# State-space loop of a hybrid decoder: TensorE adds the real part of the turned products, the fraction stays at the head of a tile, sample products come last

## The reference

```python
bu_re = einsum("btgc,gpc->btgp", u, bb_re)        # inputs to states
bu_im = einsum("btgc,gpc->btgp", u, bb_im)
s_t   = a * s_(t-1) + bu_t                        # complex, a = mag * exp(i * phi), by associative_scan
y     = einsum(s_re, c_re) - einsum(s_im, c_im) + d_skip * u
out   = gelu(y) * sigmoid(gelu(y) @ w_glu + b_glu)
```

## Time and profile before

| | |
|---|---|
| median of the runs | 3801.35 us (3799.45 to 3801.61) |
| the profiled execution | 3798.16 us, its span 3796.3 us |
| PE busy | 2867.0 us (76% of the span), 10568 instructions |
| DVE busy | 2406.9 us (63%), 3337 instructions |
| POOL busy | 1986.9 us (52%) |
| ACT busy | 656.7 us (17%) |
| the state-space loop | first fraction in the loop's form at 43.05 us, last y started at 355.92 us |
| VectorE's eight scans a tile (L1367), 128 in all | 88.8 us, 762 ns each |

### The profile page before, as it was taken

How to read it: one execution, slowest core, us unless ns; L and a number is a source line. 1 busy time by engine, 2 the same in 40 slices (tenths; PEclk the granted TensorE clock), 3 DMA queues, 4 the chain that set the end, 5 groups by cost and what they waited for, 6 DMA issues and landing times.

```text
span 3796.3 us, 30116 instructions
## 1 busy us (share of the span) xinstructions
PE 2867.0 (76%) x10568; PEld 1645.9 (43%) x10568; DVE 2406.9 (63%) x3337; ACT 656.7 (17%) x1576; POOL 1986.9 (52%) x1620
## 2 busy tenths in 40 slices
PE   4555996777666778898986788888877687666667
PEld 2223773333222326665753456665644342222222
DVE  7997077767775555666466675665456765555563
ACT  6664021101010111221011112221010111000000
POOL 5886025566656554344465453344355556555652
PEclk8777998998888999999998889998988899888888
DMA  2001459999999999999999999999999999999997
GB/s 98 14 12 70 138 241 410 425 422 423 426 419 422 427 427 427 420 411 417 426 427 422 427 421 420 408 420 421 426 427 422 418 411 427 427 427 427 427 427 316
DMA packets 197787, 1407.03 MB, mean 371 GB/s; under 512 B 21984, under 2 KB 26336, under 8 KB 26864
## 3 DMA queue, kind: packets, MB, share of 16 engines
q0 software_dynamic: 166064, 1208.62, 76.2%
q1 hardware_dynamic: 31296, 196.39, 12.6%
q10 hardware_dynamic: 288, 0.18, 0.0%
HBM read 1401.86 MB, written 3.24 MB: 370 GB/s over the span
## 4 chain that ended last, share of the span: by engine, by line
DMA 41%; PE 25%; POOL 15%; DVE 11%; issue 6%; ACT 2%; POOLq 0%; ACTq 0%; DVEq 0%
DMA arena<-in_v_dram,arena 25%; PE ps L704 16%; DMA arena<-in_u_dram,arena 11%; PE ps L626 7%; POOL arena L567 5%; DMA W<-in_slabs_dram 5%; POOL arena L556 4%; DVE arena L1532 3%; POOL arena L494 1%; POOL arena L496 1%; DVE X L1564 1%; POOL arena L472 1%; POOL arena L500 1%; PE ps L716 1%; DVE arena L1443 1%
## 5 line engine op out<-in xcount | busy, mean ns | idle before, releaser
L704 PE MATMUL ps<-arena 128*128 128x512 f32 x3584 | 1805.1, 661 | 650.8 <-DMA arena<-in_v_dram,arena 490.3
L1532 DVE CUSTOM_DVE_ANT_0 arena<-arena,HN 128x2048 f32<-128x2048 f32 x576 | 1311.1, 2291 | 1082.5 <-DMA arena<-in_u_dram,arena 1082.3
L567 POOL DMA_INDIRECT arena<-in_v_dram,arena x576 | 870.2, 1511 | 1202.4 <-PE ps L704 861.1
L704 PEld LDWEIGHTS ps<-arena 128*128 128x128 f32 x3584 | 736.3, 212 | 1686.6 <-issue 939.1
L556 POOL DMA_INDIRECT arena<-in_u_dram,arena x576 | 838.4, 1456 | 505.6 <-DVE arena L1532 192.6
L626 PE MATMUL ps<-HT,W 128*128 128x160 f32 (+2 forms) x3520 | 515.1, 309 | 42.6 <-DMA W<-in_slabs_dram 42.2
L626 PEld LDWEIGHTS ps<-HT,W 128*128 128x128 f32 x3520 | 483.0, 196 | 83.3 <-DMA W<-in_slabs_dram 47.7
L1095 ACT ACTIVATE arena<-arena 128x4 f32<-128x4 f32 x144 | 29.6, 205 | 2026.8 <-DVE arena L1532 2026.7
L1564 DVE SCALAR_TENSOR_TENSOR X<-arena,X 128x2048 f32<-128x2048 f32 x128 | 300.9, 2351 | 69.7 <-DMA arena<-in_v_dram,arena 39.3
L626 PE MATMUL ps<-arena,W 128*128 128x160 f32 (+2 forms) x1440 | 238.8, 329 | 18.0 <-DMA W<-in_slabs_dram 18.0
L626 PEld LDWEIGHTS ps<-arena,W 128*128 128x128 f32 x1440 | 213.7, 197 | 46.4 <-DMA W<-in_slabs_dram 19.9
(11 more groups left out here) (230 smaller groups left out, 1937.2 us busy)
## 6 DMA issues: line engine op xcount, KB each, us to landing
W<-in_slabs_dram SPq DMA_DIRECT2D x168, 1024.0 KB, 10.1
arena<-in_u_dram,arena POOLq DMA_INDIRECT x576, 15.0
arena<-in_v_dram,arena POOLq DMA_INDIRECT x576, 14.0
GB<-in_norms_dram SPq DMA_DIRECT2D x7, 1024.0 KB, 14.6
arena<-in_s_bc_dram SPq DMA_DIRECT2D x32, 128.0 KB, 2.1
X<-in_x_dram SPq DMA_DIRECT2D x3, 1024.0 KB, 7.2
GB<-in_keys_dram SPq DMA_DIRECT2D x2, 1024.0 KB, 10.5
out_y_dram<-HN SPq DMA_DIRECT2D x2, 1024.0 KB, 10.1
```

Source lines behind the costliest of these rows:

```text
L567: pool.indirect_dma_start(ring[:, HALF + r, :], None, experts_v[n // LAYER_ROUNDS], bass.IndirectOffsetOnAxis(ap=GI[:, at:at + 1], axis=0) ...
L704: mm = nc.tensor.matmul(ps[:, ACC_BANK + c, :], diag[:, slot, :], ring[:, HALF + r, BANK * c:BANK * (c + 1)], start=first and r == 0, stop ...
L1532: V.tensor_tensor_reduce(ring[:, r, :], ring[:, r, :], HN[:, tile_of(n), :], 1.0, 0.0, ALU.mult, ALU.add, A8[:, n % TURN, r:r + 1]).then_i ...
```

## The change

In the recurrence's input the real part was the sum of two products, added by VectorE. Now VectorE only makes the two products (M[0], M[1]) and TensorE adds them by two products with the identity into the PSUM banks where re stood; VectorE scans the real part from PSUM. The imaginary part is subtracted and scanned first, in SBUF. The order of the four turned products changes accordingly. `s5_bur` is now raised behind the scans from PSUM and not behind the four products. TensorE's `s5_out_part` is split: token products first, without the wait for the sample states, then the new sums of the next tile, then the gate sums, and the sample products last, behind the wait for `s5_bsd`. The fraction keeps its place at the head of the tile. The two scan results move from M[1] and M[3] to M[0] and M[3].

```diff
@@ TensorE
-            def s5_out_part(k, h):
+            def s5_sums(k):
+                pe.wait_ge(s5_turned, k + 1)
+                for e in range(2):
+                    nc.tensor.matmul(ps[:, e, :], ident[:], M[0][:, 2 * e:2 * e + 2, :], start=True, stop=False)
+                    mm = nc.tensor.matmul(ps[:, e, :], ident[:], M[1][:, 2 * e:2 * e + 2, :], start=False, stop=True)
+                mm.then_inc(s5_sum, 1)
+
+            def s5_out_tokens(k, h):
                 pe.wait_ge(s5_dd, k + 1)
                 pe.wait_ge(s5_cn, k + 1)
                 pe.wait_ge(s5_p, k + 1)
-                pe.wait_ge(s5_bsd, k + 1)
                 pe.wait_ge(s5_yg, k)
...
+            def s5_out_samples(k, h):
+                pe.wait_ge(s5_bsd, k + 1)
                 for n in range(2):
...
             s5_in_part(0, 0)
+            s5_sums(0)
             s5_in_part(0, 1)
-            s5_out_part(0, 0)
+            s5_out_tokens(0, 0)
+            s5_sums(1)
+            s5_out_samples(0, 0)
             for i in range(1, KT // 2):
                 for h in range(2):
                     s5_in_part(i, h)
-                    s5_out_part(2 * i + (h - 1), 1 - h)
+                    s5_out_tokens(2 * i + (h - 1), 1 - h)
+                    s5_sums(2 * i + h)
                     gate_sums(2 * i + (h - 2))
-            s5_out_part(KT - 1, 1)
+                    s5_out_samples(2 * i + (h - 1), 1 - h)
+            s5_out_tokens(KT - 1, 1)
+            s5_out_samples(KT - 1, 1)
             gate_sums(KT - 2)
@@ VectorE, s5_tile
-                V.tensor_tensor(M[0], re, cos, ALU.mult)
                 V.tensor_tensor(M[1], im, sin, ALU.mult)
-                V.tensor_tensor(M[2], im, cos, ALU.mult)
-                V.tensor_tensor(M[3], re, sin, ALU.mult).then_inc(s5_bur, 1)
-                dve.wait_ge(s5_bur, k + 1)
-                V.tensor_tensor(M[0], M[0], M[1], ALU.add)
+                if not first:
+                    dve.wait_ge(s5_p, k)
+                V.tensor_tensor(M[3], re, sin, ALU.mult)
+                V.tensor_tensor(M[0], re, cos, ALU.mult).then_inc(s5_turned, 1)
+                settle(V.tensor_tensor(M[2], im, cos, ALU.mult))
                 settle(V.tensor_tensor(M[2], M[2], M[3], ALU.subtract))
-                for src, dst in ((M[0], M[1]), (M[2], M[3])):
+                def scans(src, dst):
                     for q in range(QK):
                         ins = V.tensor_tensor_scan(dst[:, q, :], dec[:, bass.ds(k * QK + q, 1)].to_broadcast([P, SEQ]),
                                                    src[:, q, :], 0.0, ALU.mult, ALU.add)
-                settle(ins)
+                    return ins
+                scans(M[2], M[3])
+                dve.wait_ge(s5_sum, k + 1)
+                scans(re, M[0]).then_inc(s5_bur, 1)
+                dve.wait_ge(s5_bur, k + 1)
```

More of the change, by code:

```diff
@@ L348, in hybrid_step @@
         s5_sf, stores = sem("s5_sf"), sem("stores")
+        s5_turned, s5_sum = sem("s5_turned"), sem("s5_sum")
         y_stored, pool_go = sem("y_stored"), sem("pool_go")
@@ L1368, in s5_tile @@
                                                    src[:, q, :], 0.0, ALU.mult, ALU.add)
-                settle(ins)
+                    return ins
[3 more added lines that the diff above has]
+                dve.wait_ge(s5_bur, k + 1)
                 if not first:
                     dve.wait_ge(s5_y, k)
-                V.tensor_tensor(PR[0], cos, M[1], ALU.mult)
+                V.tensor_tensor(PR[0], cos, M[0], ALU.mult)
                 V.scalar_tensor_tensor(PR[1], sin, -1.0, M[3], ALU.mult, ALU.mult)
-                V.tensor_tensor(PR[2], sin, M[1], ALU.mult)
+                V.tensor_tensor(PR[2], sin, M[0], ALU.mult)
                 V.tensor_tensor(PR[3], cos, M[3], ALU.mult).then_inc(s5_p, 1)
```

## The result

The changed kernel takes 3768.43 us (median of 5 runs, 3764.73 to 3770.77) where the kernel before took 3799.77 (5 runs): a ratio of 0.991 (95% interval 0.9899 to 0.9921), 31 us less. The profiled execution took 3770.77 us, its span 3768.9.

What follows compares the result with a forecast made beforehand. The state-space loop was taken to run at VectorE's pace. Minus 21.4 us for tiles 1 to 15, plus 1.5 at tile 0, minus 2.0 at the end gave minus 21.9: 3779 us, own range 3772 to 3787, full range 3767 to 3797.

Steps and rivals of the forecast that it cites:

- first rival: In the loop, GpSimd takes over as the bound: 18.9 us a tile, 3794 us whole; chance 15 percent.
- The scans from PSUM: Four of VectorE's eight scans a tile now read PSUM: 0.26 us gained in a late tile, none in an early one.
- tile 0: First tile of the loop: VectorE waits for sums made at TensorE's low clock, plus 1.5 us.
- the tail: Loop's end: token products go ahead of TensorE's wait for GpSimd, minus 2 us.
- The addition: VectorE loses it and saves its start-to-start time: 1.35 us in a late tile, 1.15 in an early one.
- another 0.47 us: VectorE's products back could fall from 5.07 us to four times 1.15 with GpSimd further on.
- fourth rival: VectorE and GpSimd come free of each other: 17.6 us a tile, 3772 us whole; chance 8 percent.
- nine late and six early tiles: Tiles 1 to 15: minus 1.61 us for each late one, minus 1.15 for each early one, minus 21.4 in all.
- The PSUM source: By the Trainium skill's fixed cycles, 120 against 58, the 64 scans would lose an estimated 4.1 us.
- TensorE's sums: Four identity products a tile, 3.5 us at the high clock, lie beside VectorE's work with 1.7 us of slack.
- second rival: TensorE's clock stays at 1.2 GHz through the new gaps: 21.8 us a tile, 3837 us whole; chance 10 percent.
- third rival: Gain swallowed behind the loop, where the first gate product waits for a weight slab: 3795 to 3801 us; chance 8 percent.

Runs made afterwards that it cites:

- b_no_add: The kernel before with VectorE's addition of the two real products left out: 18.51 us a tile, 3788.48 us whole.
- b_one_step: The kernel before with GpSimd doing one of the four sample steps: 18.99 us a tile, 3789.08 us whole.
- a_scan_sbuf: The changed kernel with the real part scanned from SBUF, order, waits and TensorE sums kept: 18.51 us a tile, 3783.54 us whole.
- a_scan_sbuf_one_step: The changed kernel with the real part scanned from SBUF and GpSimd doing one of four sample steps: 17.85 us a tile, 3778.8 us whole.
- b_add_scan_psum: The kernel before, addition kept but its result unread, real part scanned unturned from PSUM: 18.87 us a tile, 3789.75 us whole.
- b_scan_psum: The kernel before without the addition and without TensorE sums, real part scanned unturned from PSUM: 17.62 us a tile, 3771.62 us whole.
- a_double_sums: The changed kernel with its four sums on TensorE done twice: 19.69 us a tile, 3803.9 us whole.
- b_split: The kernel before with only TensorE's order changed, sample products behind the gate sums: 19.54 us a tile, 3798.17 us whole.
- a_one_step: The changed kernel with GpSimd doing one of the four sample steps: 17.50 us a tile, 3768.74 us whole.

## Why the prediction was wrong, and what of it held

**The direction** was right, the bound only in half. VectorE has no hole before or after. But that the loop "runs at VectorE's own pace" leaves GpSimd out, which the prediction weighs only as a bound after the change (first rival, chance 15 percent). Before the change its chain is as full as VectorE's (b_no_add, above). In the changed kernel the chain from 180 to 306 us is VectorE's:

```profile
by line: DVE arena L1385 23.3%; issue 15.6%; DVE HN L1397 7.6%; DVE arena L1381 7.4%; DVE HN L1398 6.7%; DVE HN L1399 6.7%; DVE arena L1380 6.3%; DVE arena L1375 6.3%; DVE arena L1379 6.3%; DVE arena L1378 6.3%; PE ps L809 3.1%; DVE arena L
```

GpSimd is close behind there: from 150 to 300 us it waits 0.2 us for another engine.

**The scans from PSUM are the step that failed**: "I take 0.26 us gained in a late tile, none in an early one", with the other rows of the tile held at their stretched values. Eight scans were put at 5.55 us; they take 5.04, and the four that stay in SBUF have fallen too, from half of 5.81 to 2.62. Of the 0.80 us by which the tile shown beats its forecast of 18.26, the scans have 0.51, the products back 0.22 and the subtraction 0.19, less 0.12 at the fraction and the states.

That a scan from PSUM is no dearer was right: four cost 2.42 us, undisturbed ones from SBUF 2.46. But the 0.65 us that the prediction took for an undisturbed scan was itself stretched; undisturbed it is 0.60 to 0.62. And the row was priced without GpSimd. Scans from SBUF and GpSimd's work hold each other up: eight scans take 5.8 to 5.9 us beside it (before, b_one_step, a_scan_sbuf) and 5.02 without (a_scan_sbuf_one_step), and four operations of GpSimd 3.00 us beside them and 1.47 beside products out of PSUM. So the place of four scans is worth 0.63 us a tile with the addition in place (b_add_scan_psum), 0.89 without it (b_scan_psum) and 1.08 in the changed kernel (a_scan_sbuf), where 0.26 or nothing had been put. In the sum: tiles 1 to 15 gave 29.9 us, not 21.4. These 8.5 are most of the 9.1 us by which the loop beat its forecast (30.95 against 21.9); tile 0 adds 1.4 and the tail takes 0.8 back.

**The addition** was priced at 1.35 us late and 1.15 early, 1.27 in the mean of fifteen tiles. With scans from SBUF it is worth 0.99 us, with scans from PSUM 1.25: the size held within 0.3. Between the two kernels with light GpSimd and scans from SBUF (18.99 and 17.85, the latter with the sums on TensorE) it is 1.14, but that agreement is in part luck: the scans fall there too, from 5.88 to 5.02, and the products back grow by 0.33, because GpSimd's remaining work lies elsewhere in the tile.

**Step by step**, on one path from before to the changed kernel: the sample steps left out 0.51 (19.50 to 18.99), the addition moved 1.14 (to 17.85), the place of the scans 0.35 (to 17.50), the sample steps again, which now cost nothing, 0.07 (to 17.43). By this path 0.93 of the 2.07 us a tile are not the addition, by that over b_no_add 1.08. The steps are those of whole tiles; single operations do not follow them.

**The rivals.** The prediction had seen this mechanism, as "another 0.47 us" for the products back and as the fourth rival: both engines free of each other, 17.6 us a tile, chance 8 percent. At 17.43 it came nearest, in part by luck. Its own terms add up to 17.44 (18.26 less 0.35 at the scans and 0.47 at the products back), and the rows reach 17.46 otherwise: scans 5.04 us instead of 5.20, products back 4.85 instead of 4.60. The engines are not free of each other either: a sample operation beside a product back still takes 1.42 us (214.35 us). The first rival, 18.9 us with GpSimd as the bound, had 15: it is what the addition alone gives (b_no_add, 18.51, its chain all GpSimd). The two are one mechanism, and four scans decide between them.

The sentence cited at the first rival from the Trainium skill ("SBUF — State Buffer", "Who interferes with whom"), that an instruction with one SBUF input does not contend with GpSimd, agrees with the scans too: 0.32 us beside them (212.07 us). Its other half is that two SBUF inputs do contend with a GpSimd instruction that reads SBUF. The trace agrees (3.00 us beside scans from SBUF, 1.47 beside products out of PSUM). The forecast should have applied it to the scans of the kernel before: with their place alone 0.8 of GpSimd's 16.8 us a tile go, with the addition alone 0.9.

The split into nine late and six early tiles fell as well: after the change there is no slow phase, from the fifth tile on the tiles alternate between about 17.45 and 17.7.

**The PSUM source.** By the Trainium skill ("VectorE: DVE Perf Modes", section on the TRN2 errata) the scans would be an estimated 0.26 us a tile dearer, 4.1 us in all. Measured, 2.42 against 2.46 us shows nothing of it.

**TensorE's sums** lie beside VectorE's work as worked out: cover 1.4 us, forecast 1.7. The rows after (TensorE):

```profile
206.80 1.13 PE L819 MATMUL ps<-arena,ident 128*128 128x512 f32 x2 [1.73 <-DVE arena L1379]
...
209.48 1.02 PE L820 MATMUL ps<-arena,ident 128*128 128x512 f32 x2
210.34 1.68 PE L853 MATMUL ps<-arena,W 128*128 128x288 f32 x8
...
214.45 1.96 PE L809 MATMUL ps<-arena 128*128 128x512 f32 x4 [1.80 <-DVE arena L1385]
```

The sums start as soon as the third product is there and end at about 210.5, the scans that need them start at 211.92.

**The second rival**, a clock that stays low through the new gaps, went the other way: the granted clock (100 to 200 and 200 to 300 us) goes from 0.79 and 0.77 to 0.93 and 0.96, and without the sums it is 0.80 and 0.84 (b_scan_psum). Late sums, brought about by doubling them, cost what such a stall should (a_double_sums).

**Tile 0** was put at plus 1.5 us and came to plus 0.1. Its rows after, VectorE and TensorE:

```profile
54.24 2.42 DVE L1385 TENSOR_TENSOR_SCAN arena<-arena,ps 128x256 f32<-128x256 f32 x4 [1.57 <-PE ps L820]
```

```profile
56.80 3.65 PE L809 MATMUL ps<-arena 128*128 128x512 f32 x4 [2.39 <-DVE arena L1385]
```

VectorE waits 1.57 us for the sums, most of them at the low clock (granted 0.56 from 47.6 to 54.2 us; forecast 2.1), and the input products behind them are in time, at 62.6, where up to 1.5 had been allowed.

**The tail** was put at minus 2.0 and came to minus 1.2: the split gives 2.26 (b_split), and of that the same products, at the clock that rises later, take 1.0 back.

**The stage behind the loop** moved along as forecast: 30.95 us at the first gate product, 31 in the medians. The third rival is out. In the one profiled execution the span is 27.4 us shorter; the changed kernel's runs spread by 6 us, so no cause is sought for that.

Open stays where in VectorE's tile GpSimd's work comes to lie, and so how the disturbance divides operation by operation: every edit moves it. No run had GpSimd entirely still, and that the 0.35 us which scans from SBUF cost with one sample step left are the rest of it is not shown.

## What to carry to other kernels

Where two engines stretch each other, the saving of an instruction is not its row: first price the tile with one of them quiet, then ask whether the edit lets the other go or leaves it as the new bound. An engine that is busy 86 percent has no room if the rest are waits for its own last instruction. An edit that moves an operand out of the contested memory can be worth nearly as much as the instruction that it was made for, though undisturbed it costs the same from either memory. And a sum moved to an idle engine is free only as far as its cover goes: here 1.4 us, which half a subtraction more used up.

## What the runs showed of the hardware

- GpSimd's four operations on input matrices took 4.24 us beside addition, subtraction and first scans from SBUF (before), 3.00 beside scans from SBUF (b_no_add) and 1.47 beside products out of PSUM (changed).
- Undisturbed, four scans of 256 columns take 2.46 us from SBUF and 2.42 from PSUM (a_one_step). Eight from SBUF take 5.83 and 5.88 us beside GpSimd's work (a_scan_sbuf, b_one_step) and 5.02 with next to nothing of it (a_scan_sbuf_one_step).
- With the sums added to TensorE's tile the clock that it was granted rose: 0.79 and 0.77 before (100 to 200 and 200 to 300 us), 0.93 and 0.96 with them, 1.00 with twice as many.
